# Two parts of one kernel rearranged: the compression product with its operands exchanged, and the second attention with its values product at a pair's end and its rows scaled by GpSimd

## The chip, the core and the metric

The kernel runs on one core of one Trainium2 chip. The metric is device time in microseconds (us), start to end of one execution. Before the change it is 2379.49 us, the median of three runs (2378.72 to 2380.01).

The core has five engines with instruction streams of their own: TensorE (PE in the rows; its weight loads are PEld), VectorE (DVE), ScalarE (ACT), GpSimd (POOL) and SyncE (SP, which here only starts transfers). They meet at semaphores.

## The reference

Two blocks follow one another on 512 tokens with 1024 features. The first is a convolution mixer with an MLP, then a sparse attention (compressed, selected and window branch) with an MLP. The second runs a state space scan and a sliding window attention side by side, and a gated feed forward net. Two pieces of it matter here. The compression of keys and values in the first block:

```python
def compress_blocks(t, pe, w1, w2):
    chunks = t.reshape(B, S // CMP_STRIDE, CMP_STRIDE, G, dh)
    blocks = jnp.concatenate([chunks[:, :-1], chunks[:, 1:]], axis=2) + pe[None, None, :, None, :]
    flat = jnp.moveaxis(blocks, 2, 3).reshape(B, n_cmp, G, CMP_BLOCK * dh)
    return jax.nn.silu(flat @ w1) @ w2
```

With 4 groups and 31 blocks, `flat` has 124 rows of 2048 numbers, and `w1` is 2048 x 256, once for keys and once for values. And the second block's attention, 16 heads in 8 pairs, each query block of 128 looking at its own and the previous 128 keys, at 16 meta tokens and at a sink:

```python
    p = jax.nn.softmax(jnp.concatenate([s_meta, s_band, sink], axis=-1), axis=-1)
    out = (jnp.einsum('bnkgqm,bmkd->bnqkgd', p_meta, v_meta)
           + jnp.einsum('bnkgqs,bnskd->bnqkgd', p_band, vband))
```

## The kernel before, in words

**Dense products.** All weights stream in as units of 128 x 2048 numbers, two at a time in `raw`, `whi` and `wlo`. ScalarE rounds a unit to its high part `whi`, VectorE forms the low part `wlo = raw - whi` (`split_low`), and TensorE makes three products (high by high, high by low, low by high). A unit's buffer comes free when TensorE has used the unit before last, so while TensorE works on one unit the next but one is split.

**The compression product** lies between the query units: q0, phi0, q1, phi1, q2, phi2, q3, phi3. Before the change phi0 and phi1 are the two halves of the hidden features of the keys, phi2 and phi3 those of the values. `compression(c)` takes 16 tiles of 128 x 128 weights as the stationary operand and streams the 124 columns of `phi_k` or `phi_v`, three products each: 48 matmuls a unit. VectorE copies the 128 x 124 result to `hid`, ScalarE applies SiLU (for the values four times, into the zeroed rows of `hidv`), and `compressed_keys` and `compressed_blocks` multiply by `w2`.

**Start of the first attention.** After phi3 TensorE does `scores(0)`, `compressed_blocks`, `scores(1)`, then rounds n = 0, 1, ...: `turn(n)` (transposes of the probabilities), `scores(n + 2)`, values. For one round VectorE adds the bias and takes the row maxima (`scores`), ScalarE takes the exponentials (`exps`), VectorE the reciprocals of the sums (`sums`), GpSimd scales the rows (`weighed`, L542), and TensorE turns them. VectorE forms the low parts of the queries (`query_low`, 128 x 512 each, six after q3) before its first `scores`: three of them before it waits for phi3, three behind that.

**The second attention** goes over 8 pairs of heads (i, p). A pair has rows n = 0 to 7 (query block 1 + n // 2, head n % 2) and a small row 8. TensorE's order within a pair: two dense steps, then for each n: two dense steps (`dense`, six matmuls of 258 columns each; three for n = 0), `scores(n + 2)`, from n = 3 on `values(n - 1)`, and `turn(n)`. `values` multiplies by 128 stationary columns, the 64 value columns of a block beside 64 zero columns from `vals2`, so that a head's result falls on its own half of the partitions. VectorE's order for each n is written out by hand: `softmax_out(n)` (reciprocal and scaling of the row), `softmax_in(n + 2)` (bias and maximum), `turned(n)` (copy of the turned row from PSUM), and behind it now and then a piece of other work: half a `split_low` (for n = 1, 2 in pairs with p odd, for n = 4, 5 with p even), at n = 0 the low part of the last pair's result, at n = 3 and n = 6 one operation each on the gates. `turn(n)` waits for `p2_ready`, the scaled row.

GpSimd has, in this stage, only the scaling of `X` (8 operations at L629), which is used after the attention.

Of the kernel before, what the change touches and what calls it, by code (L numbers as in the profile page):

```python
# [27 lines left out]
P = 128  # L28
# [141 lines left out]
def program(nc, io):  # L170

    ctx = ExitStack()
    with ctx:
# [12 lines left out]
        acc = sb("acc", [P, TOK])  # L186
        sq = sb("sq", [P, 2, TOK])
# [35 lines left out]
        with ExitStack() as scope:  # L223
# [6 lines left out]
            with ExitStack() as part:  # L230
                hid = sb("hid", [P, 2, 2, GROUPS, CMP_PAD], F32, part)
                hidv = sb("hidv", [P, 2, GROUPS, QT, CMP_PAD], F32, part)
# [29 lines left out]
        with ExitStack() as rest:  # L262
# [28 lines left out]
            with ExitStack() as scope:  # L291
# [8 lines left out]
                vals2 = sb("vals2", [P, 2 * QT + 1, DH], F32, scope)  # L300
# [12 lines left out]
                rsum2 = sb("rsum2", [P, 4], F32, scope)  # L313
# [200 lines left out]
        def _(pool):  # L514
# [81 lines left out]
            for i in range(2):  # L596
# [14 lines left out]
                for r in range(1, 29):  # L611
# [6 lines left out]
                    if c < NC - 2:  # L618
                        pool.wait_ge(h_new, i * 8 + (4 * gg + c + 1))
                        if gg + c == 0:  # L620
# [4 lines left out]
                                                decay, ALU.mult).then_inc(hd_ready, 1)  # L625
            pool.wait_ge(x_new, KT)
# [6 lines left out]
        def _(act):  # L633
# [7 lines left out]
            def next_unit(layer, c, m=2, turn=0, half_turn=0):  # L641


                act.wait_ge(mt_full, turn * m + (T0[layer] + m * (c + 1)))
                u = U0[layer] + c + 2
                split_high(u % 2, half_turn + u // 2, unit_cols(u))

# [213 lines left out]
            for c in range(4):  # L861
                if c < 3:
                    next_unit(f"q{c}", 0)
# [13 lines left out]
                act.wait_ge(mt_free, T0[f"phi{c}"] + 1)  # L877
                h = hid[:, c // 2, c % 2, :, 0:N_CMP]
                if c < 2:
                    nc.scalar.activation(h, h, ACT.Silu).then_inc(hid_ready, 1)  # L880
                for t in range(QT if c >= 2 else 0):
                    nc.scalar.activation(hidv[:, c % 2, :, t, 0:N_CMP], h, ACT.Silu).then_inc(hid_ready, 1)
# [150 lines left out]
            for i in range(2):  # L1033
                for p in range(4):
                    base = i * 40 + 10 * p

                    def exps(n):

                        for h in range(2 if n == 8 else 1):
                            act.wait_ge(ttr2, base + (n + h + 1))  # L1040
                            if n < 8:
                                row, x, k = Pb[:, n, 0 if n > 1 else P:], P, n % 2
                            else:
                                row, x, k = Pb0[0:N_META, h, :], N_META, 2 + h
                            nc.scalar.activation(row, row, ACT.Exp, bias=nmax2[0:x, k:k + 1], scale=-1.0,
                                                 accum_out=rsum2[0:x, k:k + 1]).then_inc(exp2, 1)
# [76 lines left out]
        def _(pe):  # L1123
            def unit(layer, c, rhs, m_tiles=2, k_tiles=KT, turn=0, turn_m=2, ready=None, free=None, beside={}, read=None, halved=False):
# [3 lines left out]
                if halved:  # L1128
                    pe.wait_ge(front_lo, 2)
                else:  # L1130
# [6 lines left out]
                for ks in ((range(EARLY), range(EARLY, k_tiles)) if ready else (range(k_tiles),)):  # L1137
                    for m in range(m_tiles):
                        out = ps[:, 2 * s + m, :]
                        for k in ks:  # L1140
                            if ready and not m:
                                pe.wait_ge(*ready(k))
                            if (m, k) in beside:
                                beside[m, k]()
                            at = slice((k * m_tiles + m) * P, (k * m_tiles + m + 1) * P)
# [118 lines left out]
            def compression(c):  # L1264
# [11 lines left out]
                mm.then_inc(mt_full, 1)  # L1276

            def compressed_keys():
# [4 lines left out]
                for m in range(2):  # L1283
                    mm = nc.tensor.matmul(ps[:, 4, 0:GROUPS * CMP_PAD], w2[:, m, 0:P], hid[:, 0, m, :, :].rearrange("p g n -> p (g n)"), start=m == 0, stop=m == 1)
                mm.then_inc(cmp_full, 1)

            def compressed_blocks():

                pe.wait_ge(hid_ready, 2 + 2 * QT)
                for g in range(GROUPS):  # L1290
                    for m in range(2):
                        blocks = hidv[:, m, g, :, :].rearrange("p t n -> p (t n)")
                        mm = nc.tensor.matmul(ps[:, 5, g * DH:(g + 1) * DH], blocks, w2[:, m, P:P + DH], start=m == 0, stop=m == 1)
# [81 lines left out]
            def values(n):  # L1375


                g, h, branch = of_round(n)
                if not branch:
# [15 lines left out]
            for c in range(4):  # L1395
                unit(f"q{c}", 0, H1, free=T0[f"q{c}"] - 1)
# [207 lines left out]
            for i in range(2):  # L1604
# [7 lines left out]
                for p in range(4):  # L1612
# [34 lines left out]
                    def turn_meta():  # L1647
                        pe.wait_ge(pm_ready, i * 4 + (p + 1))
# [1184 lines left out]
```

## Time and profile before

| | |
|---|---|
| median of three runs | 2379.49 us |
| the profiled execution's own time | 2378.88 us |
| its span in the trace | 2377.0 us |
| TensorE / VectorE / ScalarE / GpSimd busy | 99% / 62% / 37% / 8% |
| granted TensorE clock over the span | 0.998 |

The profile is of one execution; the 1.9 us between its time and its span lie around the traced work. In the timeline a row has the start, the length and the count of like instructions; the length of a matmul row includes the pipeline behind the last one, so the time that a run of matmuls takes is read from the start of the run to the start of what follows. A float32 matmul that is not rounded first stands as two records.

### The profile page before, as it was taken

How to read it: one execution, taken by the hardware profiler on the slowest of the kernel's cores; microseconds unless marked ns; L12 is line 12 of the kernel's file. 1: busy time of each engine (PE TensorE's matmuls, PEld its weight loads, DVE VectorE, ACT ScalarE, POOL GpSimd, SP SyncE). 2: the span in 40 equal slices, each digit the busy share in tenths (PEclk: the TensorE clock that was granted, in tenths of full speed). 3: DMA queues.
4: the chain of work that ended last, by engine and by line, in shares of the span. 5: the costliest groups of instructions: out<-in, count | busy, mean ns of one | idle time of the engine just before them, and what ended most of it. 6: DMA issues, size and time to landing. Idle time of an engine off the chain costs nothing.

```text
span 2377.0 us, 35716 instructions
## 1 busy us (share of the span) xinstructions
PE 2353.0 (99%) x14579; PEld 2054.0 (86%) x14579; DVE 1473.5 (62%) x2592; ACT 875.7 (37%) x1390; POOL 182.5 (8%) x259
## 2 busy tenths in 40 slices
PE   9999999999999999999999999999999999999998
PEld 7888888888887778888889999999999999998997
DVE  6555344355657745444468977886766656873784
ACT  4123222233448832212245772773333333222212
POOL 0000000000038700000002200210100000000000
PEclk9999999999999999999999999999999999999999
DMA  5236223424343212222224522542222122223223
GB/s 176 89 101 153 89 91 130 135 88 125 120 127 77 72 61 99 89 93 101 88 89 122 117 85 89 122 112 89 79 80 76 61 91 93 100 89 124 89 95 118
DMA packets 67622, 239.13 MB, mean 101 GB/s; under 512 B 22482, under 2 KB 33170, under 8 KB 43634
## 3 DMA queue, kind: packets, MB, share of 16 engines
q1 hardware_dynamic: 31044, 200.14, 24.9%
q0 software_dynamic: 5952, 18.44, 4.1%
q10 hardware_dynamic: 30496, 18.73, 3.5%
q8 instruction: 93, 1.52, 0.3%
q14 instruction: 37, 0.30, 0.0%
HBM read 228.41 MB, written 10.09 MB: 100 GB/s over the span
## 4 chain that ended last, share of the span: by engine, by line
PE 88%; DVE 7%; issue 2%; ACT 2%; POOL 1%; DMA 0%; DVEq 0%; SPq 0%; ACTq 0%; POOLq 0%
PE ps L1147 44%; PE ps L1443 25%; PE ps L1733 5%; PE ps L1554 4%; DVE wlo L1788 1%; POOL Sb L542 1%; PE ps L1662 1%; PE ps L1390 1%; PE ps L1372 1%; PE ps L1274 1%; PE ps L1317 1%; PE ps L1636 1%; PE ps L1212 0%; ACT Sb L893 0%; PE ps L1505 0%
## 5 line engine op out<-in xcount | busy, mean ns | idle before, releaser
L639 ACT ACTIVATE whi<-raw 128x2048 fp32r<-128x2048 f32 (+2 forms) x185 | 345.7, 1869 | 854.7 <-PE ps L1147 451.3
L1788 DVE TENSOR_TENSOR wlo<-raw,whi 128x2048 fp32r<-128x2048 f32 (+3 forms) x210 | 417.9, 1990 | 71.9 <-ACT whi L639 71.6
L1147 PE MATMUL ps<-parts,whi 128*128 128x512 f32 x1328 | 418.0, 396 | 0.7 <-DVE ct L1930 0.7
L1443 PE MATMUL ps<-parts,whi 128*128 128x258 f32 (+1 forms) x2400 | 403.2, 290 | 1.1 <-issue 0.8
L1443 PEld LDWEIGHTS ps<-parts,whi 128*128 128x128 f32 x2400 | 331.2, 189 | 11.4 <-issue 10.0
L1147 PEld LDWEIGHTS ps<-parts,whi 128*128 128x128 f32 x1328 | 248.2, 188 | 61.8 <-issue 3.3
L1147 PE MATMUL ps<-parts,wlo 128*128 128x512 f32 x664 | 262.5, 395 | 0.0
L1443 PE MATMUL ps<-parts,wlo 128*128 128x258 f32 (+1 forms) x1200 | 242.5, 284 | 0.0
L1147 PE MATMUL ps<-Mlo,whi 128*128 128x512 f32 x512 | 203.0, 396 | 0.0
L1147 PE MATMUL ps<-Mhi,whi 128*128 128x512 f32 x512 | 203.0, 396 | 0.0
L1147 PE MATMUL ps<-Mhi,wlo 128*128 128x512 f32 x512 | 203.0, 396 | 0.0
L1443 PEld LDWEIGHTS ps<-parts,wlo 128*128 128x128 f32 x1200 | 185.9, 189 | 0.0
L1443 PE MATMUL ps<-AThi,whi 128*128 128x258 f32 x832 | 168.4, 284 | 0.2 <-DVE GA L2524 0.2
L1443 PE MATMUL ps<-AThi,wlo 128*128 128x258 f32 x832 | 168.0, 284 | 0.0
L1443 PE MATMUL ps<-ATlo,whi 128*128 128x258 f32 x832 | 167.0, 282 | 0.0
L1147 PEld LDWEIGHTS ps<-parts,wlo 128*128 128x128 f32 x664 | 124.8, 188 | 29.0
L1877 DVE TENSOR_TENSOR X<-X,ps 128x512 f32<-128x512 f32 x64 | 43.9, 686 | 154.6 <-PE ps L1147 154.6
L1443 PEld LDWEIGHTS ps<-AThi,whi 128*128 128x128 f32 x832 | 129.5, 190 | 0.5 <-DVE GA L2524 0.3
L1443 PEld LDWEIGHTS ps<-ATlo,whi 128*128 128x128 f32 x832 | 128.9, 189 | 0.0
L1443 PEld LDWEIGHTS ps<-AThi,wlo 128*128 128x128 f32 x832 | 128.5, 189 | 0.0
L1147 PEld LDWEIGHTS ps<-Mhi,wlo 128*128 128x128 f32 x512 | 96.4, 188 | 23.5
L1147 PEld LDWEIGHTS ps<-Mlo,whi 128*128 128x128 f32 x512 | 96.4, 188 | 23.5
(419 smaller groups left out, 3930.7 us busy)
## 6 DMA issues: line engine op xcount, KB each, us to landing
raw<-in_stream SPq DMA_DIRECT2D x186, 1024.0 KB, 4.8
csb<-sums_d POOLq DMA_DIRECT2D x16, 512.0 KB, 6.0
bands<-scratch ACTq DMA_DIRECT2D x7, 1024.0 KB
csf<-sums_d POOLq DMA_DIRECT2D x32, 128.0 KB, 6.0
tabs<-bands ACTq DMA_DIRECT2D x8, 418.0 KB, 4.2
X<-in_x SPq DMA_DIRECT2D x4, 512.0 KB, 7.5
near_a<-bands ACTq DMA_DIRECT2D x8, 256.0 KB, 2.6
Q_odd<-parts POOLq DMA_DIRECT2D x8, 256.0 KB, 4.4
```

Of the source, the lines that this page charges most:

```text
L542: nc.gpsimd.tensor_scalar(row, row, rsum[:, n % 2, t:t + 1], gates[:, t, at:at + 1], ALU.mult, ALU.mult).then_inc(probs_ready, 1)
L639: nc.scalar.activation(whi[:, s, 0:cols], raw[:, s, 0:cols], ACT.Copy).then_inc(hi_done, 1)
L1147: mm = nc.tensor.matmul(out, w[:, s, at], x(k), start=k + j == 0, stop=k == k_tiles - 1 and j == 2)
L1274: mm = nc.tensor.matmul(ps[:, 2 * s, 0:GROUPS * N_CMP], w[:, s, at], x[:, part, k, :], start=k + j == 0, stop=k == 15 and j == 2)
L1317: mm = nc.tensor.matmul(ps[:, bank, at:at + (t + 1) * P], Qst[g % 2][:, h, t * P:(t + 1) * P], Ks[g % 2][:, part, branch, 0:(t + 1) * P], ...
L1372: mm = nc.tensor.transpose(ps[:, bank, at:at + P], Sb[:, n % 2, first(t) + k * P:first(t) + (k + 1) * P], ident)
L1390: mm = nc.tensor.matmul(ps[b * DH:(b + 1) * DH, 6, k * P:SEQ], Vt[:, branch, k, g * DH:(g + 1) * DH], PT[b][:, at:at + w], start=False, st ...
L1443: mm = nc.tensor.matmul(ps[:, 2 * par + h, 0:w], wt[:, s, at], x[:, k, a + h * w:a + (h + 1) * w], start=k + j == 0, stop=k == k_tiles - 1 ...
L1554: mm = nc.tensor.matmul(ps[:, 4 * (r % 2) + 2 * gg + h, 0:LATE // 2], w[:, s, at], x[:, k, CUT + h * LATE // 2:CUT + (h + 1) * LATE // 2], ...
L1733: mm = nc.tensor.matmul(ps[:, 2 * (t % 2) + bank, 0:w], wt[:, u % 2, at], x[:, k, x0:x0 + w], start=k + j == 0, stop=k == b - a - 1 and j ...
L1788: low = nc.vector.tensor_tensor(wlo[:, s, a:b], raw[:, s, a:b], whi[:, s, a:b].bitcast(F32), ALU.subtract)
L1877: nc.vector.tensor_tensor(x, x, ps[:, 2 * ((U0[layer] + j) % 2) + m, :], ALU.add).then_inc(mt_free, 1)
```

## The change

**Compression.** The operands change places: the 124 columns of `phi` become the stationary operand and 256 weight columns stream, so that a unit takes 24 matmuls instead of 48. Units are cut along the contraction: phi0 and phi1 add into one result for the keys, phi2 and phi3 for the values. The result has the hidden features along its rows (`hrow`, 124 x 256), so after SiLU TensorE turns it (`hidden_turned`, two transposes: for the keys within unit q2, for the values between `scores(0)` and `scores(1)`) and VectorE copies it on (`hidden_copied`). `hidv` now lies in the memory of `acc` and `sq`. `compressed_blocks` moves behind `turn(0)` and `scores(2)`, and VectorE's `values_compressed` behind its `scores(2)`. The unit that follows a phi unit is split in two halves (`next_halves`, `split_low(..., halved=True)`), and TensorE waits for the first half only. All six `query_low` of the last units come after the copy of phi3's result.

**Second attention.** `vals2` holds each block's 64 columns once, without zeros. `values()` runs once, at the pair's end: for each block two matmuls of 64 stationary columns, one for each head, into the two halves of the partitions. VectorE gives only the reciprocal (one column of `rsum2` for each row), and GpSimd scales all 64 rows, before it scales `X`.

```diff
@@ compression(c)
-                for k in range(16):
-                    at = slice(k * P, (k + 1) * P)
+                for n in range(KT):
+                    k, at = KT * (c % 2) + n, slice(n * PHI, (n + 1) * PHI)
                     for j, (w, part) in enumerate(((whi, 0), (whi, 1), (wlo, 0))):
-                        mm = nc.tensor.matmul(ps[:, 2 * s, 0:GROUPS * N_CMP], w[:, s, at], x[:, part, k, :],
+                        mm = nc.tensor.matmul(ps[0:GROUPS * N_CMP, 2 * s, 0:PHI], x[:, part, k, :], w[:, s, at],
                                               start=k + j == 0, stop=k == 15 and j == 2)
                 mm.then_inc(mt_full, 1)
+            def hidden_turned(kv, bank):
+                pe.wait_ge(hid_ready, 2 * kv + 1)
...
+                for m in range(2):
+                    mm = nc.tensor.transpose(ps[:, bank, m * P:m * P + rows], hrow[:, m * P:(m + 1) * P], ident[0:rows, 0:rows])
+                mm.then_inc(cmp_full, 1)
@@ TensorE, start of the first attention
             scores(0)
-            compressed_blocks()
+            hidden_turned(1, 6)
             scores(1)
-            pe.wait_ge(cmp_ready, 2)
             for n in range(ALL_ROUNDS):
                 turn(n)
                 if n + 2 < ALL_ROUNDS:
                     scores(n + 2)
+                if n == 0:
+                    compressed_blocks()
@@ VectorE, query and compression units
+                if c < 3:
+                    dve.wait_ge(front_hi, 4 + c)
+                    split_low(f"q{c}", 0, part=0, halved=True)
+                    dve.wait_ge(hi_done, U0[f"q{c}"] + 3)
+                    split_low(f"q{c}", 0, part=1)
...
-                for k in range(2, KT - 3 if c == 3 else 0):
-                    query_low(k)
                 dve.wait_ge(mt_full, T0[f"phi{c}"] + 1)
-                nc.vector.tensor_copy(hid[:, c // 2, c % 2, :, 0:N_CMP],
-                                      ps[:, 2 * (U0[f"phi{c}"] % 2), 0:GROUPS * N_CMP].rearrange("p (g n) -> p g n", g=GROUPS)).then_inc(mt_free, 1)
+                if c % 2:
+                    nc.vector.tensor_copy(hrow[:, :], ps[0:GROUPS * N_CMP, 2 * (U0[f"phi{c}"] % 2), 0:PHI]).then_inc(mt_free, 1)
+                else:
+                    nc.vector.memset(step[:, :], 0.0).then_inc(mt_free, 1)
...
-            for k in range(KT - 3, KT):
+            for k in range(2, KT):
                 query_low(k)
@@ GpSimd, second attention
+            for n in range(8 * 2 * QT):
+                row = Pb[:, n % 8, 0 if n % 8 > 1 else P:]
+                pool.wait_ge(sums_ready, ALL_ROUNDS + n + 1)
+                nc.gpsimd.tensor_scalar(row, row, rsum2[:, n % 8:n % 8 + 1], None, ALU.mult).then_inc(p2_ready, 1)
@@ VectorE, softmax_out(n)
-                        c = rsum2[:, n % 2:n % 2 + 1]
-                        own.mark(nc.vector.reciprocal(c, c))
-                        own.wait()
-                        row = Pb[:, n, 0 if n > 1 else P:]
-                        nc.vector.tensor_scalar(row, row, c, None, ALU.mult).then_inc(p2_ready, 1)
+                        c = rsum2[:, n:n + 1]
+                        nc.vector.reciprocal(c, c).then_inc(sums_ready, 1)
@@ TensorE, second attention
-                    def values(n):
-                        pe.wait_ge(pt2_dve, base + (n + 1))
...
-                        for block in range(c - 2, c if c == QT else c - 1):
+                    def values():
+                        pe.wait_ge(pt2_dve, base + 8)
...
+                        for block in range(QT):
                             w = 2 * P if block < QT - 1 else P
-                            mm = nc.tensor.matmul(ps[:, 7, block * P:block * P + w], vals2[:, 2 * block + 1 - h:2 * block + 3 - h, :].rearrange("p a d -> p (a d)"),
-                                                  PT2[:, h, 2 * block * P:2 * block * P + w], start=n == 2, stop=False, skip_group_check=True)
+                            for h in range(2):
+                                nc.tensor.matmul(ps[h * DH:(h + 1) * DH, 7, block * P:block * P + w], vals2[:, block, :],
+                                                 PT2[:, h, 2 * block * P:2 * block * P + w], start=block == 0, stop=False, skip_group_check=True)
```

VectorE around row n = 2 of a pair with p odd, before the change (`Pb` is the row, `PT` the turned row, `ps` is PSUM, `wlo<-raw,whi` is half a `split_low`):

```order
L2487 COPY PT<-ps 128x128
L1788 TENSOR_TENSOR wlo<-raw,whi 128x1024
L2478 RECIPROCAL rsum<-rsum 128x1
L2481 TENSOR_SCALAR Pb<-Pb,rsum 128x273
L2459 MEMSET step 128x1
L2466 ISA Pb,nmax<-ps,tabs 128x273
L2466 ISA nmax 128x1
L2487 COPY PT<-ps 128x256
```

The same place after it:

```order
L2537 COPY PT<-ps 128x128
L1820 TENSOR_TENSOR wlo<-raw,whi 128x1024
L2531 RECIPROCAL rsum<-rsum 128x1
L2512 MEMSET step 128x1
L2519 ISA Pb,nmax<-ps,tabs 128x273
L2519 ISA nmax 128x1
L2537 COPY PT<-ps 128x256
```

The scaling has left VectorE; the half split still stands ahead of the reciprocal, and the copy of the turned row still ahead of the half split.

TensorE for row n = 4 of a pair before (`parts` are dense steps, `keys,Q` is `scores(6)`, `PT,vals` is `values(3)`, `consts,Pb` is `turn(4)`):

```order
L1443 MATMUL ps<-parts,whi 128x258 x4
L1443 MATMUL ps<-parts,wlo 128x258 x2
L1443 MATMUL ps<-parts,whi 128x258 x4
L1443 MATMUL ps<-parts,wlo 128x258 x2
L1636 MATMUL ps<-keys,Q 128x273
L1662 MATMUL ps<-PT,vals 128x256
L1644 MATMUL ps<-consts,Pb 128x128
L1645 MATMUL ps<-consts,Pb 128x128
```

and after:

```order
L1474 MATMUL ps<-parts,whi 128x258 x4
L1474 MATMUL ps<-parts,wlo 128x258 x2
L1474 MATMUL ps<-parts,whi 128x258 x4
L1474 MATMUL ps<-parts,wlo 128x258 x2
L1667 MATMUL ps<-keys,Q 128x273
L1675 MATMUL ps<-consts,Pb 128x128
L1676 MATMUL ps<-consts,Pb 128x128
```

The values product is gone from between `scores` and `turn`; all eight of its matmuls stand together at the pair's end.

VectorE ahead of the first attention's second round, after the change (`parts<-Qall,parts` is `query_low`, `Sb,nmax` are the four pieces of `scores`, `acc_sq<-ps` is `hidden_copied`, `cst` are the sums of the compressed branch):

```order
L2116 TENSOR_TENSOR Sc<-Sc,cst 128x512
L2177 COPY hrow<-ps 124x256
L2057 TENSOR_TENSOR parts<-Qall,parts 128x512 x6
...
L2067 COPY acc_sq<-ps 128x16x31
L2067 COPY acc_sq<-ps 128x16x31
L2121 TENSOR_REDUCE cst<-Sc 128x16
L2123 RECIPROCAL cst<-cst 128x16
L2127 TENSOR_TENSOR cst<-cst,gates 128x16
L2096 RECIPROCAL rsum<-rsum 128x4
```

Before, three of the six `parts` rows stood ahead of the copy of phi3's result, and no `acc_sq` rows stood there.

## Rows read from the trace of the kernel before

**Rows 1.** The page: busy time of each engine, share, instructions.
```profile
PE 2353.0 (99%) x14579; PEld 2054.0 (86%) x14579; DVE 1473.5 (62%) x2592; ACT 875.7 (37%) x1390; POOL 182.5 (8%) x259
```

**Rows 2.** Timeline of TensorE: first matmuls of phi0, and first behind it.
```profile
640.30 0.44 PE L1274 MATMUL ps<-phi_k,whi 128*128 128x124 f32 x2
...
645.71 0.68 PE L1147 MATMUL ps<-parts,whi 128*128 128x512 f32 x2
```

**Rows 3.** Timeline of TensorE near the end: matmuls of 256 columns, 26 apart.
```profile
2357.79 0.28 PE L1733 MATMUL ps<-Fhi,wlo 128*128 128x256 f32 x1
...
2360.87 0.28 PE L1733 MATMUL ps<-parts,whi 128*128 128x256 f32 x1
```

**Rows 4.** Timeline of TensorE: the product of compressed_blocks.
```profile
699.42 1.89 PE L1293 MATMUL ps<-w,hidv 128*128 128x64 f32 x16
```

**Rows 5.** Timeline of TensorE: values(7) of the first pair, and what follows.
```profile
1704.92 0.82 PE L1662 MATMUL ps<-PT,vals 128*128 128x256 f32 x4
1705.57 0.27 PE L1649 MATMUL ps<-consts,Pmeta 128*128 128x128 f32 x1
```

**Rows 6.** Timeline of TensorE: first attention, 64 stationary columns for each of two heads.
```profile
713.94 0.49 PE L1390 MATMUL ps<-PT_a,Vt 128*64 128x384 f32 x1
713.94 0.49 PE L1390 MATMUL ps<-PT_b,Vt 128*64 128x384 f32 x1
...
714.58 0.27 PE L1390 MATMUL ps<-PT_a,Vt 128*64 128x128 f32 x1
```

**Rows 7.** Timeline of TensorE in the second pair, from turn(2) to scores(6).
```profile
1718.79 0.33 PE L1644 MATMUL ps<-consts,Pb 128*128 128x128 f32 x1 [0.35 <-DVE Pb L2481]
...
1720.50 0.62 PE L1636 MATMUL ps<-keys,Q 128*128 128x273 f32 x2
1720.96 0.59 PE L1662 MATMUL ps<-PT,vals 128*128 128x256 f32 x2
1721.39 0.29 PE L1644 MATMUL ps<-consts,Pb 128*128 128x128 f32 x1
...
1723.06 0.62 PE L1636 MATMUL ps<-keys,Q 128*128 128x273 f32 x2
```

**Rows 8.** Timeline of VectorE in the same pair.
```profile
1718.18 0.16 DVE L2478 RECIPROCAL rsum<-rsum 128x1 f32<-128x1 f32 x1
...
1719.27 0.43 DVE L2487 COPY PT<-ps 128x256 f32<-128x256 f32 x1 [0.16 <-PE ps L1645]
1719.61 1.22 DVE L1788 TENSOR_TENSOR wlo<-raw,whi 128x1024 fp32r<-128x1024 f32 x1
1720.74 0.16 DVE L2478 RECIPROCAL rsum<-rsum 128x1 f32<-128x1 f32 x1
...
1722.17 0.68 DVE L2546 TENSOR_TENSOR sq<-ps,R 128x516 f32<-128x516 f32 x1
1722.77 0.15 DVE L2478 RECIPROCAL rsum<-rsum 128x1 f32<-128x1 f32 x1
```

**Rows 9.** Groups of instructions of GpSimd: scaling of rows in the first attention.
```profile
L542 POOL TENSOR_SCALAR Sb<-Sb,rsum,gates 128x256 f32<-128x256 f32 x32 | 17.6, 550 | 0.0
```

**Rows 10.** The chain in order of time, start of the first attention.
```profile
697.00 0.68 PE ps L1274 x6
...
703.17 0.19 DVE rsum L2052
...
703.46 2.38 POOL Sb L542 x4
...
705.89 0.89 PE ps L1372 x4
```

**Rows 11.** Timeline of VectorE: the last three low parts of the queries.
```profile
697.91 1.88 DVE L2024 TENSOR_TENSOR parts<-Qall,parts 128x512 fp32r<-128x512 f32 x3
```

**Rows 12.** Stages: busy us of each engine, granted clock, DMA share, GB/s.
```profile
702.60:706.40 3.80, 1.84 (x11) 1.16 (x11) 3.48 (x17) 2.83 (x10) 2.58 (x5) 0.97 0.96 217
706.40:709.70 3.30, 3.30 (x15) 3.00 (x14) 2.44 (x9) 2.48 (x8) 3.22 (x6) 0.52 0.65 151
```

More of the change, by code:

```diff
@@ L646, in next_unit, with next_halves @@
                 split_high(u % 2, half_turn + u // 2, unit_cols(u))
+            def next_halves(layer):
+                act.wait_ge(mt_full, T0[layer] + 2)
+                u = U0[layer] + 2
+                act.wait_ge(landed[u % 2], u // 2 * 16 + 16)
+                for half, done in enumerate((front_hi, hi_done)):
+                    cols = slice(half * FRONT, (half + 1) * FRONT)
+                    nc.scalar.activation(whi[:, u % 2, cols], raw[:, u % 2, cols], ACT.Copy).then_inc(done, 1)
             def norm_tile(n, part, k, slot, gain, after, a=N_META, hi=Hhi):
@@ L876, in _ @@
                     query_high(k)
[L877 to L882, printed above, removed]
+                if c % 2:
+                    act.wait_ge(mt_free, T0[f"phi{c}"] + 1)
+                    nc.scalar.activation(hrow[:, :], hrow[:, :], ACT.Silu).then_inc(hid_ready, 1)
                 if c == 1:
@@ L1123, in _, with unit @@
         def _(pe):
-            def unit(layer, c, rhs, m_tiles=2, k_tiles=KT, turn=0, turn_m=2, ready=None, free=None, beside={}, read=None, halved=False):
+            def unit(layer, c, rhs, m_tiles=2, k_tiles=KT, turn=0, turn_m=2, ready=None, free=None, beside={}, read=None, halved=False, half=0):
                 s = (U0[layer] + c) % 2
@@ L1129, in unit @@
                     pe.wait_ge(front_lo, 2)
+                elif half:
+                    pe.wait_ge(front_lo, half)
                 else:
@@ L1144, in unit @@
                                 beside[m, k]()
+                            if half and (m, k) == (0, KT // 2):
+                                pe.wait_ge(lo_done, U0[layer] + c + 1)
                             at = slice((k * m_tiles + m) * P, (k * m_tiles + m + 1) * P)
@@ L1395, in _ @@
             for c in range(4):
-                unit(f"q{c}", 0, H1, free=T0[f"q{c}"] - 1)
+                unit(f"q{c}", 0, H1, free=T0[f"q{c}"] - 1, half=c and 2 + c, beside={(0, KT - 2): lambda: hidden_turned(0, 5)} if c == 2 else {})
                 if c == 2:
@@ L1691, in _ @@
                     turn_first()
-                    values(7)
+                    dense(1)
                     turn_meta()
-                    dense(2)
+                    dense(1)
                     values_first()
+                    values()
                     values_meta()
@@ L1778, in _, with split_low @@
             own = Link(dve, dve_own)
-            def split_low(layer, c, turn=0, part=None):
+            def split_low(layer, c, turn=0, part=None, halved=False):
                 u = U0[layer] + c + 2
@@ L1785, in split_low @@
                 a, b = (0, cols) if part is None else (part * cols // 2, (part + 1) * cols // 2)
-                if a == 0:
+                if a == 0 and not halved:
                     dve.wait_ge(hi_done, turn + (u + 1))
@@ L1790, in split_low @@
                     low.then_inc(lo_done, 1)
+                elif halved:
+                    low.then_inc(front_lo, 1)
             def norm_tile(n, part, k, slot, gain, a=N_META, hi=Hhi, lo=Hlo):
@@ L2146, in _ @@
                     scores(n + 2)
+                if n == 0:
+                    values_compressed()
                 if n and n % 4 == 0:
```

80 lines of the change are left out of this document (49 added, 31 removed).

## The prediction

> **What bounds the kernel now.** I read the page first. TensorE is busy 99% of the span [rows 1]. So an edit can gain only by taking time out of TensorE's own stream, and it gains nothing where the freed time turns into a wait. I therefore priced each edit on TensorE from starts in its timeline, and then looked, at both places, for what TensorE would wait for next: in the second attention in the timelines of TensorE and VectorE side by side, at the first attention's start in the chain in order of time.
>
> **The compression product.** Unit phi0 runs from 640.30 to 645.71 us [rows 2]: 5.41 us for 48 matmuls, 0.113 us each, though each streams only 124 columns. 128 weight columns are loaded for every one of them, and that sets the pace: compressed_blocks streams 64 columns and goes no faster, (1.89 - 0.27) / 15 = 0.108 us [rows 4]. Matmuls of 256 streamed columns come every (2360.87 - 2357.79) / 26 = 0.1185 us [rows 3]. 24 of those are 2.84 us. Four units: 4 x (5.41 - 2.84) = 10.3 us less. The two transposes of the keys within q2 are new, some 0.3 us with the change of operands; those of the values fall where TensorE waits anyway. First term: -10.0 us.
>
> The Trainium skill (TensorE: Matmul & The Clock Gate, section on FWL and DoubleRow) says that a fast weight load needs exactly 128 weight columns and an input that is not float32. 124 columns would lose it. By that rule, if it held for the rounded operands here, the loads would get slower and the term would shrink. The row speaks against it: the loads of plain float32 weights in compressed_blocks, which the rule excludes, come as fast (0.108 us) as the rounded ones of phi0 (0.113 us), so there seems to be nothing to lose. It stays a rival below.
>
> Does the halved split hold? When q0 ends, ScalarE's split of a whole unit takes 1.9 us and VectorE's 2.3 us, 4.2 us in turn, which hides under a phi unit of 5.4 us and would not under 2.84. With halves TensorE needs about 0.95 + 1.22 us (half a split in [rows 8]) and some 0.2 us, 2.4 us in all, ahead of the 2.84. I cost it at nothing; without it 1.4 us would come back three times.
>
> **The start of the first attention.** Here phi3 had a second use: it covered three `query_low`. Phi3's last matmul drains at 697.68 [rows 10], three `query_low` take 1.88 us [rows 11], and the reciprocal of round 0 comes at 703.17, 5.5 us behind phi3. That round was paced by ScalarE and by `values_compressed`. After the change VectorE copies `hrow` (0.35 us as the 256-column copy in [rows 8] up to the next instruction) and does six `query_low` (3.76 us), so the round's `scores` begin 4.1 us behind phi3. Its four pieces (1.6 us) and the last exponential (about 0.95 us) bring the reciprocal to 6.8 us, 1.3 us later than now relative to phi3. For round 1 VectorE has `scores` (1.75), the two new copies of 496 columns (1.25) and the compressed sums (1.1), then GpSimd 1.05 + 2.4 us. The last transposes of `turn(1)` end near 15 us behind phi3, against 13.3 us now. That is 1.7 us.
>
> The clock adds to it. TensorE was busy 1.84 of 3.80 us, and then the granted clock stood at 0.52, which is the 1.2 GHz level, for 3.3 us [rows 12]. After the change the idle stretch is longer (from `scores(0)` to `turn(0)` TensorE has only `scores(1)` to do), so the fall is almost sure, and `compressed_blocks` (1.7 us), which now fills idle time, will stand behind `turn(0)` where the clock is low. Work of 0.43 + 1.36 + 1.7 + 0.43 + 1.07 = 5.0 us (last transposes of `turn(0)`, `scores(2)`, blocks, compressed transposes, `turn(1)`) starts 9.5 us behind phi3. If the clock is low until about 13.2 us, as long behind dense work as now, 1.85 us of it are done by then and it ends at 16.3. Second term: between +1.7 and +3.1, I take +2.9 us. What follows is paced by TensorE as now.
>
> Compression part: -10.0 + 2.9 = -7.1 us, between -8.4 and -4.5.
>
> **The values product.** `values(7)` takes 0.65 us for a product of 256 and one of 128 columns [rows 5], so 256 columns cost 0.43 and 128 cost 0.22. A pair has six of the one and two of the other: 3.0 us. In the first attention two products with 64 stationary columns start at the same time, 713.94 twice, and both of 384 columns are through at 714.58, that is 0.64 us [rows 6], what one costs alone at four cycles a column of the 2.4 GHz clock (0.64 us). So two heads go at the price of one, and the pair's values take 1.5 us and perhaps 0.1 us to change over. Third term: 8 x (-1.5 + 0.08) = -11.3 us.
>
> **What TensorE then waits for.** Between two turns TensorE has turn and two dense steps, 1723.06 - 1721.39 = 1.67 us, scores, 1720.96 - 1720.50 = 0.46 us, and values 0.43 us [rows 7]: 2.56 us. Without values 2.13 us. Against that stands a loop: `turn(n)`, VectorE's copy of the turned row, whatever stands behind it, the reciprocal of row n + 1, its scaling, `turn(n + 1)`. From [rows 7, 8]: turn at 1718.79, copy at 1719.27 (0.48 us), half split at 1719.61 (0.34), reciprocal at 1720.74 (1.13). From the reciprocal at 1718.18 to the turn at 1718.79 it is 0.61 us now. With a half split the loop is 0.48 + 0.34 + 1.13 + 0.61 = 2.56 us, exactly what TensorE has to do. So the values product was what covered it.
>
> By GpSimd the last leg is longer. Reciprocal to GpSimd's start is 0.29 us [rows 10], 256 columns take 0.55 us [rows 9], so 273 some 0.56, and 0.04 to 0.06 us pass to the transposes [rows 10]: 0.91 us, 0.30 more than now. The loops become
> - with a half split 2.86 us against 2.13: TensorE waits 0.73. Where only the small scores (0.14 us) stand between, in pairs with p even at n = 5, it is against 1.81: 1.05.
> - with the gate operation (0.60 us, [rows 8]) at n = 3: 2.33 to 2.43 against 2.13: 0.2 to 0.3. At n = 6, with no scores ahead: 2.33 against 1.67: 0.66.
> - at n = 0, with the low part of the last result: about 0.16. With nothing behind the copy 1.73: no wait.
>
> A pair with p odd waits 0.16 + 0.7 + 0.73 + 0.2 + 0.66 = 2.45 us, one with p even 0.16 + 0.3 + 0.73 + 1.05 + 0.66 = 2.9 us, 21.4 us for all eight. Now it is 0.5 us in odd pairs (TensorE could have turned at 1718.28) and about 0.25 in even ones, 3.0 us. Fourth term: +18.4 us, less 0.3 us in the first pair, where the scaling of `X` moves out of the way. Behind the turns nothing is late: the copy of row 7 ends 1 us after `turn(7)`, and `values()` comes 2.5 us after it. The scaling of `X` (10.3 us) moves behind the last row, with 46 us of products ahead of its use.
>
> Second attention: -11.3 + 18.4 - 0.3 = +6.8 us. The price that I could not read is the last leg with one scalar instead of two. Lower bound 0.61 us, VectorE's own: then the waits are 4 x (1.3 + 1.7) = 12 us, and the part gives -11.3 + 12 - 3 - 0.3 = -2.6. Upper bound 1.0 us (0.14 us to the first transposes, as after an idle stretch): +10. I take 0.91, as its three pieces are measured on the same chain in the first attention.
>
> **Sum.** 2377.0 - 7.1 + 6.8 = 2376.7 us of span, 2378.6 us of time for an execution like the profiled one. That one lies 0.6 us below the median of its runs, so for the median I say 2379.0 us: two changes that cancel.
>
> **The rivals.**
> - Faster: GpSimd's leg costs little more than VectorE's. For it speaks that one scalar is read instead of two; against it the 0.29 us of handing over, which no shape changes. With -2.6 and -7.1 the time is 2369.8 us. Chance 0.2, with the milder cases down to 4.7 us saved.
> - Slower, the clock: the waits of an even pair lie close together (0.73, 1.05 and 0.66 in 9 us, 27% of the time idle), and if the granted clock falls there as it did at 706.4 after 52% idle, each fall costs half of 3.3 us, 1.6 us a pair: +13 us, 2392 us. It decides from three falls on. Against it: much less idle than in [rows 12]. Chance 0.12.
> - Slower, the loads: 124 weight columns load at half the pace, 0.2 us each. The compression then gains nothing, -0.1 instead of -10.3: 2389 us. Chance 0.05.
> - Slower, contention: GpSimd's scaling runs beside VectorE's bias and copy operations. The Trainium skill (GPSIMD Engine Reference, key points) says that the two share SBUF interfaces, and names instructions of VectorE with two SBUF inputs. In this order the half split comes ahead of the reciprocal, so it never runs beside GpSimd; only if the loop broke that order would it cost. Chance 0.06, at +1 us a pair, 2387 us.
>
> **The numbers.** Changes within 0.2% (4.75 us) can't be told from none here. The likeliest case gives 2379.0, its own range 2374 to 2384 from the two parts' bounds taken apart. The chances: faster 0.2, within 0.2% 0.57, slower 0.23. For 8 in 10 the range must reach into the rivals on both sides, 2371 to 2388.
>
> **What the trace will show.** Right: phi units of 2.8 us; the reciprocal of round 0 some 6.8 us behind phi3; a low clock of 3 us or more behind `turn(0)`; eight values matmuls in 1.5 us at a pair's end; waits of 0.7 us at the turns behind a half split and behind n = 6, released by GpSimd; pair periods of 27.3 us or a little more, against 27.3 now. Wrong: 0.6 us from a reciprocal to its turn; a phi unit near 5 us; a clock below 1.00 in the pairs; a wait at the transposes of the keys within q2, whose cover I worked out as only 0.3 us.

## The result, and the profile after

The changed kernel takes 2397.88 us (median of 4 runs, 2397.73 to 2399.41), beside 2379.75 us for the kernel before on the same chip (4 runs): 1.0075 times as long, with a 95% interval of 1.0063 to 1.0087. I had said 2379.0. The profiled execution is the one of 2399.41 us, the slowest of the four and 1.5 us above their median; its span is 2397.6 us.

The page of the changed kernel, busy time of each engine, to be held against [rows 1], and its chain by engine:

```profile
PE 2344.2 (98%) x14487; PEld 2033.5 (85%) x14487; DVE 1453.2 (61%) x2533; ACT 874.4 (36%) x1385; POOL 241.6 (10%) x323
...
PE 81%; DVE 9%; issue 3%; POOL 3%; ACT 2%; DMA 1%; SPq 0%; DVEq 0%; ACTq 0%; POOLq 0%
```

TensorE has 8.8 us less to do and the span is 20.6 us longer: the time went into waits. To find the stage, compare the long stretches of the chain in order of time (start, length), which do the same work in both kernels. Of the kernel before:

```profile
895.69 346.45 PE ps L1147 x1485
...
1998.25 129.94 PE ps L1443 x1080
```

and of the changed kernel:

```profile
889.97 346.45 PE ps L1163 x1485
...
2018.83 129.96 PE ps L1474 x1080
```

The first begins 5.7 us earlier than before, the second 20.6 us later. So the first half gained, and 26.3 us were lost between them, where only the second attention differs.

**The first half.** TensorE's timeline of the changed kernel, phi0 and what follows it, phi3's last matmul, and the first 128-column product of the first attention, which answers to the last row of [rows 6]:

```profile
641.20 0.50 PE L1290 MATMUL ps<-whi,phi_k 128*124 128x256 f32 x2
...
644.17 0.62 PE L1163 MATMUL ps<-parts,whi 128*128 128x512 f32 x2
...
688.54 0.28 PE L1290 MATMUL ps<-wlo,phi_v 128*124 128x256 f32 x1
...
708.56 0.27 PE L1420 MATMUL ps<-PT_a,Vt 128*64 128x128 f32 x1
```

A phi unit takes 2.97 us. From phi0's start to the drain of phi3's last matmul it is 47.6 us (641.20 to 688.82), against 57.4 (640.30 to 697.68, [rows 2, 10]): 9.8 less. From there to the product named it is 19.7 us against 16.9: 2.8 more. The stages of that start (length, busy time of PE, PEld, DVE, ACT and POOL, then the granted clock; the DMA's share and GB/s end the line):

```profile
690.70:693.60 2.90, 0.39 (x3) 0.14 (x1) 2.86 (x10) 1.40 (x5) 0.42 (x1) 1.00 0.00 0
693.60:696.40 2.80, 2.62 (x9) 1.90 (x9) 1.88 (x11) 2.34 (x10) 2.51 (x6) 0.53 0.70 142
696.40:699.00 2.60, 2.54 (x10) 1.63 (x11) 2.60 (x7) 1.90 (x8) 1.84 (x3) 0.50 0.95 214
699.00:701.10 2.10, 2.10 (x10) 2.05 (x10) 2.03 (x11) 1.33 (x5) 1.34 (x2) 0.61 1.02 231
701.10:703.30 2.20, 2.20 (x21) 2.16 (x21) 1.18 (x5) 1.83 (x7) 2.12 (x5) 1.00 0.45 76
```

After 2.9 us in which TensorE was busy for 0.39, it works at 0.50 of its clock (the 1.2 GHz level) for some 7 us.

**The second attention.** The waits of TensorE by line and releaser (us in total, times, longest), against 1.7 us in all at these transposes before:

```profile
PE ps L1675 <- POOL Pb L631: 25.4, 36, 1.2
```

TensorE's timeline in the second pair, which answers to [rows 7]:

```profile
1714.83 0.62 PE L1667 MATMUL ps<-keys,Q 128*128 128x273 f32 x2
1716.21 0.33 PE L1675 MATMUL ps<-consts,Pb 128*128 128x128 f32 x1 [0.76 <-POOL Pb L631]
...
1717.92 0.62 PE L1667 MATMUL ps<-keys,Q 128*128 128x273 f32 x2
1719.44 0.33 PE L1675 MATMUL ps<-consts,Pb 128*128 128x128 f32 x1 [0.90 <-POOL Pb L631]
```

and VectorE's and GpSimd's rows just ahead of the first of these turns:

```profile
1714.93 0.16 DVE L2531 RECIPROCAL rsum<-rsum 128x1 f32<-128x1 f32 x1
```
```profile
1715.19 0.97 POOL L631 TENSOR_SCALAR Pb<-Pb,rsum 128x273 f32<-128x273 f32 x1 [2.01 <-DVE rsum L2531]
```

From the reciprocal to the turn it is 1.28 us, where I had 0.91: the handing over takes 0.26 us, as expected, but the scaling 0.97 instead of 0.56. The groups of GpSimd show that this is no single case (busy us, mean ns of one):

```profile
L631 POOL TENSOR_SCALAR Pb<-Pb,rsum 128x273 f32<-128x273 f32 x48 | 46.6, 971 | 82.0 <-DVE rsum L2531 82.0
...
L544 POOL TENSOR_SCALAR Sb<-Sb,rsum,gates 128x512 f32<-128x512 f32 x32 | 24.5, 764 | 0.0
...
L544 POOL TENSOR_SCALAR Sb<-Sb,rsum,gates 128x256 f32<-128x256 f32 x32 | 17.6, 550 | 0.0
...
L631 POOL TENSOR_SCALAR Pb<-Pb,rsum 128x145 f32<-128x145 f32 x16 | 10.4, 652 | 196.1 <-DVE rsum L2531 196.1
```

(971 - 652) / 128 = 2.5 ns a column, against (764 - 550) / 256 = 0.84 in the first attention.

The clock stays at 1.00 through the pairs. This is the whole second pair:

```profile
1707.78:1737.65 29.87, 26.68 (x206) 23.72 (x205) 16.41 (x62) 8.48 (x23) 7.13 (x8) 1.00 0.25 85
```

In the last pair it does not. First VectorE's timeline there, then GpSimd's, then TensorE's, then two stages:

```profile
1910.21 1.29 DVE L2541 COPY Pmeta<-Pb 128x128 f32<-128x128 f32 x1 [1.10 <-POOL Pb L631]
1911.43 0.14 DVE L2525 RECIPROCAL rsum<-rsum 16x2 f32<-16x2 f32 x1
1911.61 1.08 DVE L2528 TENSOR_TENSOR Pfirst<-Pb,rsum 16x32 f32<-16x32 f32 x1
```
```profile
1910.15 6.19 POOL L635 TENSOR_TENSOR X<-X,R 128x512 f32<-128x512 f32 x5
```
```profile
1912.74 0.47 PE L1685 MATMUL ps<-consts,Pfirst 128*128 128x128 f32 x1 [1.34 <-DVE Pfirst L2528]
```
```profile
1911.60:1912.70 1.10, 0.00 (x0) 0.00 (x0) 1.09 (x2) 0.00 (x0) 1.10 (x2) 0.84 0.00 0
1912.70:1914.50 1.80, 1.76 (x8) 1.76 (x9) 0.49 (x2) 0.00 (x0) 1.80 (x2) 0.50 0.00 0
```

The scaling of `X`, which I had moved to "behind the last row" and forgotten, now starts as soon as row 7 is scaled. Beside it VectorE's copy of `Pmeta` takes 1.29 us and its `Pfirst` 1.08 us (0.23 and 0.18 us in the second pair). TensorE, already late, waits 1.34 us more, and the clock falls to 0.50 for about 6.8 us. The wait belongs to the order, the fall to this execution: with the same order of the second attention, in the run with rows of 276 numbers below, the same transpose waits as long and is not slowed,

```profile
1912.95 0.33 PE L1685 MATMUL ps<-consts,Pfirst 128*128 128x128 f32 x1 [1.35 <-DVE Pfirst L2529]
```

and the granted clock is 1.00 over the 18 us behind it, as it is in the run of the second attention's part alone. In the kernel before, these products run in the first pair, and there they slow VectorE as well: two of its row scalings of 145 columns take 1.23 and 1.31 us, for 0.30 us in the later pairs.

### The profile page after: what moved, and what is told of

Its sections match the earlier page's. It is cut to its first block, busy times and chain, and to the rows that moved or that the text cites. A ratio compares the mean times of both kernels' runs of the same rounds, so it can differ in the third digit from the quotient of the medians.

```text
span 2397.6 us, 35543 instructions
## 1 busy us (share of the span) xinstructions
PE 2344.2 (98%) x14487; PEld 2033.5 (85%) x14487; DVE 1453.2 (61%) x2533; ACT 874.4 (36%) x1385; POOL 241.6 (10%) x323
## 4 chain that ended last, share of the span: by engine, by line
PE 81%; DVE 9%; issue 3%; POOL 3%; ACT 2%; DMA 1%; SPq 0%; DVEq 0%; ACTq 0%; POOLq 0%
PE ps L1163 43%; PE ps L1474 22%; PE ps L1765 5%; PE ps L1585 3%; DVE wlo L1820 2%; POOL Pb L631 1%; POOL Sb L544 1%; DVE PT L2537 1%; PE ps L1400 1%; PE ps L1420 1%; PE ps L1695 1%; DMA raw<-in_stream 1%; PE ps L1345 1%; PE ps L1290 0%; PE ps L1675 0%
## 5 line engine op out<-in xcount | busy, mean ns | idle before, releaser
L645 ACT ACTIVATE whi<-raw 128x2048 fp32r<-128x2048 f32 (+2 forms) x182 | 340.0, 1868 | 834.5 <-PE ps L1163 427.3
```

The source lines that it names most:

```text
L645: nc.scalar.activation(whi[:, s, 0:cols], raw[:, s, 0:cols], ACT.Copy).then_inc(hi_done, 1)
```

## The experiments

Each ratio is to the runs of the kernel before that were made beside it, with its 95% interval.

**One part alone.** The second attention's hunks undone, or the compression's:

> Only the compression part, with the second attention as before. Theory A (the two parts are independent, and the whole loss sits in the second attention): the trace of the changed kernel has phi0's first matmul to phi3's last 9.8 us shorter and the stretch from there to the first values product 2.8 us longer, so about 6.7 us less, 2373. Theory B (the moved work of the start or the halved splits cost more than that stretch shows, for instance later in the MLP): 2376 or more. The groups of GpSimd stay as before.

Measured: 2373.55 us, ratio 0.9971 (0.9961 to 0.9982): 5.9 us faster than the 2379.41 of before. Theory A. The profiled execution lies 2.6 us over the median, and the reason is in its stages at the start of the first attention:

```profile
694.00:697.00 3.00, 2.97 (x9) 2.17 (x9) 2.08 (x11) 2.54 (x11) 2.72 (x6) 0.50 0.75 142
697.00:700.00 3.00, 2.93 (x13) 2.11 (x12) 2.93 (x10) 1.84 (x7) 1.63 (x3) 0.50 0.96 223
700.00:703.00 3.00, 3.00 (x13) 2.81 (x12) 2.59 (x12) 2.40 (x9) 2.87 (x5) 0.50 0.74 159
703.00:706.00 3.00, 3.00 (x16) 3.00 (x16) 0.48 (x2) 0.73 (x2) 1.59 (x2) 0.50 0.25 87
```

The same instructions as in the changed kernel, and the clock stays at 0.50 for 13.6 us instead of 6.8. Over the nine traces with this order, phi3's first matmul to the first values product took 21.3 us five times, then 21.5, 21.6, 22.0 and, here, 24.0.

> Only the second attention's part, with the compression as before. By the difference of the changed kernel and of the compression part alone it should cost 2397.9 - 2373.6 = 24.3 us: 2403.7. If the two parts disturb each other it lies outside 2402 to 2406.

Measured: 2403.21 us, ratio 1.0097 (1.0079 to 1.0115), 23.3 us slower than the 2379.89 of before. The two parts add up (-5.9 and +23.3, for +18.1 together); the loss is all in the second attention.

**What makes GpSimd slow.** Three edits of one line, or of the rows' pitch:

```diff
-nc.gpsimd.tensor_scalar(row, row, rsum2[:, n % 8:n % 8 + 1], None, ALU.mult)
+nc.gpsimd.tensor_scalar(row, row, rsum2[:, n % 8:n % 8 + 1], ones[:, 0:1], ALU.mult, ALU.mult)   # e2
+nc.gpsimd.tensor_scalar(row, row, rsum2[:, n % 8:n % 8 + 1], 1.0, ALU.mult, ALU.mult)            # e5
-Pb = sb("Pb", [P, 2 * QT, ROW], F32, scope)
+Pb = sb("Pb", [P, 2 * QT, ROW + 3], F32, scope)                                                  # e3
```

The other lines of e3 set the three new columns to zero and keep VectorE and ScalarE at 273.

> The changed kernel, but GpSimd scales each row by two scalars (the reciprocal and a column of ones), the form that the first attention has. Theory A (the form decides: with one scalar GpSimd needs 2.5 ns a column, with two 0.83): 273 columns take 0.56 us instead of 0.97, each wait at a turn gets 0.41 us shorter or vanishes, 1.7 us a pair, 14 us in all: 2384. Theory B (the shape decides: rows of 273 numbers, an odd count at odd addresses): still 0.97 us and 2398. Theory C (GpSimd is slowed by what VectorE does beside it): 0.97 us too, as VectorE does the same as in the changed kernel.

> The changed kernel, but the rows of Pb lie 276 numbers apart and GpSimd scales all 276 (the three at the end are zeros), so count and addresses are multiples of four numbers; still one scalar. Theory A (form): 0.98 us a row, 2398, nothing changes. Theory B (shape): about 0.57 us a row, 2384.

> The changed kernel, GpSimd's second factor is the constant 1.0 in the instruction instead of a column in memory. Theory A1 (what is slow is the instruction with a single operation; any second operation makes it fast): 0.57 us for 273 columns and 2382, as in the run with two columns. Theory A2 (it takes two pointers to columns to be fast): 0.97 us and 2398.

Measured: 2381.79 us with two columns (ratio 1.0005, 0.9996 to 1.0014), 2397.77 with even rows (1.0074, 1.0060 to 1.0088), 2380.49 with the constant (0.9994, 0.9985 to 1.0003). The groups of GpSimd, first of the run with two columns:

```profile
L631 POOL TENSOR_SCALAR Pb<-Pb,rsum,consts 128x273 f32<-128x273 f32 x48 | 27.6, 575 | 87.5 <-DVE rsum L2531 87.5
```

with rows of 276 and one multiplication:

```profile
L631 POOL TENSOR_SCALAR Pb<-Pb,rsum 128x276 f32<-128x276 f32 x48 | 46.8, 975 | 82.0 <-DVE rsum L2532 82.0
```

and with the constant:

```profile
L631 POOL TENSOR_SCALAR Pb<-Pb,rsum 128x273 f32<-128x273 f32 x48 | 23.8, 495 | 89.1 <-DVE rsum L2531 89.1
...
L631 POOL TENSOR_SCALAR Pb<-Pb,rsum 128x145 f32<-128x145 f32 x16 | 6.2, 388 | 198.0 <-DVE rsum L2531 198.0
```

Neither the width, nor the addresses, nor VectorE's work beside it: what is slow is the instruction with one multiplication. The work of VectorE is the same in all three runs and in the changed kernel. With a second multiplication, even by the constant 1.0, a column takes (495 - 388) / 128 = 0.84 ns instead of 2.5, and 17.4 us come back (16.1 with the column of ones, where I had expected 14).

**What the longer leg costs.** In the next run VectorE scales the rows, as before; the values product stays at the pair's end. GpSimd's loop over the rows is gone, so its scaling of `X` runs in the first pair again.

```diff
-            for n in range(8 * 2 * QT):
-                row = Pb[:, n % 8, 0 if n % 8 > 1 else P:]
-                pool.wait_ge(sums_ready, ALL_ROUNDS + n + 1)
-                nc.gpsimd.tensor_scalar(row, row, rsum2[:, n % 8:n % 8 + 1], None, ALU.mult).then_inc(p2_ready, 1)
...
-                        nc.vector.reciprocal(c, c).then_inc(sums_ready, 1)
+                        own.mark(nc.vector.reciprocal(c, c))
+                        own.wait()
+                        row = Pb[:, n, 0 if n > 1 else P:]
+                        nc.vector.tensor_scalar(row, row, c, None, ALU.mult).then_inc(p2_ready, 1)
```

> The changed kernel, but VectorE scales the rows, as before the change; the values product stays at the pair's end. If the loss is the leg from the reciprocal to the turn (1.28 us in the changed kernel, 0.61 us before), the waits fall from 4.2 us a pair to about 1.5 us: some 21 us less, 2377, and the waits left stand behind a half split. If the loss were in the values product at the end or its 64-column form, it would stay near 2398.

Measured: 2372.15 us, ratio 0.9967 (0.9954 to 0.9979): 25.7 us less than the changed kernel, 1.4 less than the compression part alone. That is 4.9 us more than I had expected; part of it is the last pair, where `X` is no longer scaled beside VectorE's operations, which the expectation left out. The waits of TensorE:

```profile
PE ps L1671 <- DVE Pb L2530: 6.7, 22, 0.5
```

So by itself the values product at the end is no loss, but of the 10.7 us that it takes off TensorE's stream all but 1.4 us go into the loop between turns.

**The loop opened.** VectorE's order alone is changed: the reciprocal of row n + 1 comes ahead of `softmax_in(n + 2)` and `turned(n)` instead of behind `turned(n)`. Once with GpSimd's slow form, once with VectorE's scaling, once in the kernel before with nothing else changed:

```diff
+                    softmax_out(0)
                     for n in range(8):
-                        softmax_out(n)
                         if n < 7:
+                            softmax_out(n + 1)
                             softmax_in(n + 2)
```

> The changed kernel with GpSimd's slow form, but VectorE gives the reciprocal of row n + 1 before its softmax_in(n + 2) and before its copy of turned row n, one row earlier. If the loss is the loop turn, copy, reciprocal, scaling, turn, it is open now: GpSimd has a whole row's time (2.1 us) for 0.97 + 0.3 us, the waits at the turns vanish, 4.2 us a pair or 33 us in all: about 2365. If GpSimd's slow operation costs by itself (what it does to VectorE or ScalarE beside it), most of the loss stays: over 2385.

> The kernel with rows scaled by VectorE and the values product at the pair's end, with reciprocal and scaling one row earlier. Its waits now are 0.9 us in odd pairs and 1.2 us in even ones by the releases, some 1.5 us with the slower first transposes; without the loop they vanish: about 2361 to 2364. If VectorE itself is the bound there (it has about 1.9 us of work for 2.13 us of TensorE's), waits move elsewhere and it stays at 2368 or more, over the run with GpSimd.

> The kernel before the change, with nothing but VectorE's reciprocal and scaling one row earlier. The loop costs it little, as the values product between the turns covers it: the waits at the turns (3.0 us by my working, 1.7 us by the releases) vanish, 2376.5 to 2378. So what the earlier row gives with the values product at the pair's end (10.7 us) is not to be had here. If it gives as much here too, 2369, my account of the cover is wrong.

Measured: 2364.91 us (ratio 0.9926, 0.9912 to 0.9940), 2361.43 us (0.9913, 0.9899 to 0.9927) and 2377.96 us (0.9987, 0.9978 to 0.9996). In the first, with the slow scaling kept, the turn stands right behind the scores, 0.46 us after their start, as if nothing had to be waited for. TensorE's timeline in the second pair:

```profile
1711.82 0.62 PE L1667 MATMUL ps<-keys,Q 128*128 128x273 f32 x2
1712.28 0.27 PE L1675 MATMUL ps<-consts,Pb 128*128 128x128 f32 x1
```

Starts of two neighbouring pairs in the run with VectorE's scaling:

```profile
1706.75 0.66 PE L1663 MATMUL ps<-keys,Q 128*128 128x145 f32 x4
...
1732.20 0.66 PE L1663 MATMUL ps<-keys,Q 128*128 128x145 f32 x4
```

25.45 us a pair, 29.87 in the changed kernel, 27.3 before. With GpSimd's slow scaling the pair from 1705.13 us takes 25.44: out of the loop, the slow form costs nothing. In the kernel before, the earlier row gives only 1.9 us, where it gives 10.7 with the values product at the end: there the product covers the loop. The 3.5 us between the medians of GpSimd's version and of VectorE's lie, by the traces, mostly where `X` is scaled. In the traces GpSimd's version has 1.5 us less in its first pair (25.51 us, against 27.00, where the scaling of `X` runs beside VectorE's). From the last pair's start to the dense products behind the attention it takes 4.1 us more (125.1 against 121.0), with this wait,

```profile
PE ps L1685 <- DVE Pfirst L2528: 2.3, 1, 2.3
```

and a granted clock of 0.91 over the 18 us from 1872 to 1890 us. In VectorE's version the last pair has no such wait, and the clock is 1.00. How much of the clock's part is only this execution's, one trace can't show.

**The start of the first attention**, and the halves, on the fastest kernel:

```diff
# e10: VectorE, and TensorE (hidden_copied and compressed_blocks taken from their places in the change)
+            hidden_copied(1, 6)
             dve.wait_ge(q_lo, KT)
             scores(0)
...
             hidden_turned(1, 6)
+            compressed_blocks()
             scores(1)
# e11: e10, and ahead of the wait for phi3
+                for k in range(2, KT - 3 if c == 3 else 0):
+                    query_low(k)
...
-            for k in range(2, KT):
+            for k in range(KT - 3, KT):
                 query_low(k)
# e12: without e10 and e11; TensorE's wait for the half and VectorE's split in two parts are undone too
-                    next_halves(f"q{c}")
+                    next_unit(f"q{c}", 0)
```

> The fastest kernel so far (2361.4 us: rows by VectorE, one row earlier), with hidden_copied of the values ahead of the first scores on VectorE, and compressed_blocks back into TensorE's idle time ahead of scores(1). Theory A (of the 2.8 us at the start of the first attention, the blocks behind turn(0) at the 1.2 GHz clock are a good part): round 0 begins 1.25 us later for the copies, 1.75 us of blocks leave the stretch, and their sums are early, so 0.5 to 2 us less, 2360. Theory B (round 0's delay decides alone): 1.2 us more, 2362.6.

> The run with the blocks in the idle time, and three query_low ahead of phi3's wait again, as before the change. VectorE idles only 0.57 us ahead of the copy of phi3's result, so that is all that it can win: 0.3 to 0.6 us less than the run without it. If the lost cover of phi3 were the larger part of the 2.8 us, as the 1.9 us of the three operations would say, 1.9 us less.

> The fastest kernel so far (2361.4 us) without the split in halves: ScalarE and VectorE split the unit behind each query unit in one piece, and TensorE waits for the whole. The two splits take 1.9 and 2.3 us in turn, a phi unit now 2.97 us. By my working 1.2 to 1.4 us come back three times: some 4 us, 2365.3. If something else covers it, 2361.4.

Measured: 2362.77 us (ratio 0.9929, 0.9916 to 0.9942), 2362.32 us (0.9924, 0.9911 to 0.9937), 2364.46 us (0.9936, 0.9924 to 0.9948). The first two can't be told from 2361.43 by their intervals; their traces take 23.4 and 23.2 us from phi3's first matmul to the first values product, which is 1.4 and 1.2 us over the 22.0 of the trace of the fastest kernel and some 2 us over the usual 21.3. In all three traces the clock is low for 10.2 us. That speaks for theory B. The three `query_low` put back give 0.4 us (0.2 in the traces), as expected from VectorE's idle 0.57 us, so the cover that phi3 lost is not the larger part of the 2.8 us. The stage in which the blocks run in the first of them:

```profile
693.90:697.30 3.40, 3.38 (x16) 3.38 (x17) 1.80 (x10) 2.29 (x8) 2.06 (x5) 0.50 0.86 204
```

They wait 3.0 us for their input, the clock is at 0.50 when it comes, and they then take 3.4 us instead of 1.7. What should have filled idle time stands in front of `scores(1)`. Without the halves TensorE waits 0.89, 1.52 and 1.05 us for the split behind phi0, phi1 and phi2:

```profile
660.68 0.73 PE L1159 MATMUL ps<-parts,whi 128*128 128x512 f32 x2 [1.52 <-DVE wlo L1816]
```

3.5 us in all, and the time is 3.0 us longer: the halves pay for themselves, by a little less than the 4 us that I had put on them.

## Why the prediction was wrong

- **Compression product, -10.0: right.** 9.8 us, with phi units of 2.97 us for the 2.84 worked out. From matmul to matmul it is 0.124 us, hardly more than the 0.1185 of 128 weight columns, so the rival of the loads falls. The Trainium skill's rule on fast loads (TensorE: Matmul & The Clock Gate, section on FWL and DoubleRow) made no difference to the time here; whether a load was of the fast kind before or after, no run shows.
- **Start of the first attention, +2.9: the sum right (2.8), its parts not.** The reciprocal of round 0 comes at 695.57, 6.75 us behind phi3's drain, where I had 6.8. But the clock falls already at `scores(1)` and stays low for 7 us, not for 3.7 behind `turn(0)`. How long it stays low differs between traces of the same order by up to 6.8 us. So it is in part luck that the sum came out: from phi3's drain to the product named above it took 19.7 to 19.8 us in five of the nine traces, and up to 22.4, and with the order of before 16.9, 16.6 and 16.3. The median of the compression part alone is 5.9 us under the kernel before, for my 7.1. Moving the blocks back did not help, so what each piece of the 2.8 us costs stays open. The bounds that I gave for this part don't follow from its terms, which give -8.3 to -6.9.
- **Values product, -11.3: right.** Eight pairs of products take 1.66 us (1702.22 to 1703.88), 10.7 us less in all.
- **The waits, +18.4: the failed step is the price of GpSimd's leg.** It takes 1.28 us. I took 0.91 us and closed its range at 1.0, because its three pieces were "measured on the same chain in the first attention". The piece of 0.56 us was measured on an instruction with two multiplications, and I read it as the price of a scaling. It is 0.97 us with one. I counted the missing scalar even in favour of speed, in the first rival. The waits, from the end of the scores to the turn, are 0.31, 0.92, 1.06, 0.51, 0.38 and 0.99 us in a pair with p odd, 4.2 us for my 2.45, and 4.3 for my 2.9 in a pair with p even: 34.0 us in all (the second and the third pair, four times) instead of 21.4. (The profile's own 25.4 us leave out waits that it doesn't mark, as the 0.31, and some 0.16 us at each marked one.) With the leg that I had assumed (the run with two columns) the waits are 2.08 and 2.65 us in such pairs, 18.9 us in all, the second part costs 2381.79 - 2373.55 = 8.2 us, against the 6.8 forecast, and the whole is 2381.8 for my 2379.0. The loop and the cover by the values product were right, and so were the places of the waits, but for one: the 0.38 us where I had none come from the longer leg and are gone with the shorter one. One duration was wrong. A row for 2.5 ns a column was in the trace before: GpSimd's scaling of `X`, 512 columns in 1.28 us. It has two inputs in memory, and I left it out as another kind. The likeliest case's own range, 2374 to 2384, was too narrow below by my own terms too: the bounds of the second part alone, -2.6 and +10, reach from 2369.6 to 2382.2, and those of the first come on top.
- **The scaling of X: a step that I costed at nothing.** I looked at who uses `X` and not at what runs beside the scaling. Beside it two of VectorE's operations take 1.06 and 0.90 us longer, and TensorE waits 1.34 us. In the profiled execution the clock falls behind that: about 1.3 + 3.4 = 4.7 us, once. In the traces of the runs with two columns, with rows of 276, with the constant and of the second attention's part alone it stays at 1.00, and about 1.3 us is all that the step costs there. What makes the clock fall in one execution and not in another stays open. The contention rival had the mechanism. The Trainium skill's statement beside it (GPSIMD Engine Reference, key points: the SBUF interfaces are shared) agrees with the row of `Pfirst`, which has two inputs in SBUF; the copy of `Pmeta` has one, and no row tells whether it ran in the other mode that the page names. But I had put it beside the row scaling, where the order of VectorE excludes it.
- **The rivals.** The clock in the pairs did not fall (1.00 in each but the last), nor did GpSimd's leg come out short. Sum in the trace: +31.0 (waits, 34.0 for 3.0), about +1.5 (a turn with the dense steps behind it takes 1.71 us after a wait, for 1.67), -10.7, +4.7: 26.5, for 26.3 measured in the profiled execution. Without the fall of the clock it is 23.1, for the 23.3 of the second attention's part alone.

## What to carry to other kernels

A duration is that of an instruction's form, not of its task: before the price of a moved operation is taken from another row, compare the number of operations and operands, and where they differ set the range by every row of that engine, the slow ones too. When work is taken out of a stream that waits on a loop, first measure the loop; here 10.7 us were to be had only after one line of another engine's order had opened it, and then GpSimd's slow scaling cost nothing in the pairs either (2397.9 to 2364.9 us). And of an operation that moves behind others, ask not only who uses its result but what it then runs beside. The best version keeps the turned compression product and the paired values at the end, scales on VectorE, and gives each row's reciprocal one row earlier: 2361.43 us, 0.9913 of the kernel before.

## What the runs showed that was not expected

- GpSimd multiplies 273 columns by one scalar in 971 ns, and by the same scalar and 1.0 in 495 ns (by a second column in 575 ns): 2.5 against 0.84 ns a column.
- A copy of 128 x 128 on VectorE takes 1.29 us instead of 0.23, and a product of 16 x 32 numbers 1.08 instead of 0.18, beside GpSimd's products of two inputs, which take 1.28 us each, as a median, there as in the kernel before.
- TensorE's clock was low for 6.8 to 13.6 us in the same stretch of the same order; the execution with the longest lies 2.6 us above the median of its kernel. And after the same wait in the last pair (1.34 or 1.35 us) it fell in one of three traces.
